# Deeper rings of split weights, shared banks combined over three tile pairs with four plain tiles last, and decay products moved from GpSimd to ScalarE in a three-block float32 model

## The reference, cut to what matters

```python
def _mlp(x, norm_g, w1, w2):              # w1: 1024 x 4096, w2: 4096 x 1024
    h = _rmsnorm(x, norm_g)
    return jnp.square(jax.nn.relu(h @ w1)) @ w2

# retention: per head a decay table, from one learned logit per head and direction
dmask = where(allowed, exp(lg * maximum(diff, 0)), 0)   # lg = log_sigmoid(decay)
a = einsum('bhid,bhjd->bhij', qc, kc) * dmask
```

## Time and profile before

| | |
|---|---|
| median of 3 runs | 979.84 us (979.39 to 979.91) |
| the profiled execution | 980.77 us, span of its instructions 979.0 us |
| mean granted TensorE clock | 0.997 |
| PE busy | 963.0 us, 98% |
| DVE busy | 776.1 us, 79% |
| ACT busy | 599.2 us, 61% |
| POOL busy | 168.5 us, 17% |
| DMA | 174.82 MB, mean 179 GB/s |

### The profile page before, as it was taken

One profiled execution on the slowest core, in us unless ns is written; L12 is line 12 of the kernel. 1 busy time (PEld: TensorE's weight loads), 2 busy tenths in 40 slices (PEclk: granted clock), 3 DMA queues, 4 the chain that ended last, 5 costly groups with the idle time before them and its releaser, 6 DMA issues.

```text
span 979.0 us, 15251 instructions
## 1 busy us (share of the span) xinstructions
PE 963.0 (98%) x5810; PEld 845.5 (86%) x5810; DVE 776.1 (79%) x1161; ACT 599.2 (61%) x987; POOL 168.5 (17%) x189
## 2 busy tenths in 40 slices
PE   9999999999998999999999999999999999999997
PEld 8878899988997888888889999998888888998885
DVE  6788678999878676786668888888767998878884
ACT  6688666556675564444447765665545867766662
POOL 2741017990000202320001000000550110000000
PEclk9999999999999999999999999999999999999999
DMA  9985545565555554435555656564545463644631
GB/s 338 302 218 194 175 129 177 182 201 194 192 175 170 189 196 154 150 130 176 189 195 172 199 176 208 193 216 145 181 161 170 133 212 94 205 133 129 215 129 44
DMA packets 110345, 174.82 MB, mean 179 GB/s; under 512 B 4289, under 2 KB 73025, under 8 KB 110273
## 3 DMA queue, kind: packets, MB, share of 16 engines
q1 hardware_dynamic: 109840, 173.40, 53.9%
q10 hardware_dynamic: 432, 0.44, 0.1%
HBM read 172.78 MB, written 1.05 MB: 178 GB/s over the span
## 4 chain that ended last, share of the span: by engine, by line
PE 90%; DVE 7%; issue 1%; ACT 0%; POOLq 0%; POOL 0%; DVEq 0%; ACTq 0%
PE ps L467 20%; PE ps L468 19%; PE ps L469 19%; PE ps L527 8%; PE ps L574 7%; PE ps L525 5%; DVE wlo L1638 3%; PE ps L543 2%; PE ps L738 1%; PE ps L718 1%; PE ps L524 1%; PE ps L541 1%; PE ps L706 1%; PE ps L662 1%; DVE arena L1765 1%
## 5 line engine op out<-in xcount | busy, mean ns | idle before, releaser
L1638 DVE TENSOR_TENSOR wlo<-raw,whi 128x1024 fp32r<-128x1024 f32 (+1 forms) x312 | 366.7, 1203 | 42.8 <-ACT whi L1105 33.1
L1105 ACT ACTIVATE whi<-raw 128x1024 fp32r<-128x1024 f32 (+1 forms) x312 | 307.2, 1023 | 41.8 <-PE ps L469 18.9
L467 PE MATMUL ps<-hT,whi 128*128 128x256 f32 x584 | 165.8, 284 | 0.3 <-issue 0.3
L469 PE MATMUL ps<-hT,wlo 128*128 128x256 f32 x584 | 165.2, 283 | 0.0
L468 PE MATMUL ps<-hT,whi 128*128 128x256 f32 x584 | 165.2, 283 | 0.0
L467 PE MATMUL ps<-whi,hT 128*128 128x512 f32 (+1 forms) x312 | 122.0, 391 | 0.9 <-DVE hT L1720 0.9
L469 PE MATMUL ps<-whi,hT 128*128 128x512 f32 (+1 forms) x312 | 120.0, 385 | 0.0
L468 PE MATMUL ps<-wlo,hT 128*128 128x512 f32 (+1 forms) x312 | 119.9, 384 | 0.0
L527 PE MATMUL ps<-hT,whi 128*128 128x512 f32 x336 | 119.8, 396 | 0.0
L467 PEld LDWEIGHTS ps<-hT,whi 128*128 128x128 f32 x584 | 111.5, 191 | 2.7 <-issue 1.4
L468 PEld LDWEIGHTS ps<-hT,whi 128*128 128x128 f32 x584 | 111.6, 191 | 1.2
(11 more groups left out here) (253 smaller groups left out, 1700.0 us busy)
## 6 DMA issues: line engine op xcount, KB each, us to landing
raw<-in_w SPq DMA_DIRECT2D x64, 1024.0 KB, 5.4
raw<-in_w_in SPq DMA_DIRECT2D x34, 1024.0 KB, 5.2
raw<-in_w_in_o SPq DMA_DIRECT2D x24, 1024.0 KB, 5.1
raw<-in_w_out_o SPq DMA_DIRECT2D x8, 1024.0 KB, 5.0
raw<-in_w_in_e SPq DMA_DIRECT2D x5, 1024.0 KB, 12.8
raw<-in_w_mem SPq DMA_DIRECT2D x4, 1024.0 KB, 10.3
raw<-in_w_out_e SPq DMA_DIRECT2D x4, 1024.0 KB, 5.0
raw<-in_w_out SPq DMA_DIRECT2D x4, 1024.0 KB, 5.0
```

Of the source, the lines that this page charges most:

```text
L467: e.matmul(o, a[0], b[0], start=start, stop=False)
L469: return e.matmul(o, a[1], b[0], start=False, stop=stop)
L1105: e.activation(split_half(i)[0], raw_half(i), ACT.Copy).then_inc(*up("hi", ("hi", i)))
L1638: e.tensor_tensor(l, raw_half(i), h.bitcast(F32), ALU.subtract).then_inc(*up("lo", ("lo", i)))
```

## The change

It does five things:

1. The rings get 7 buffers each (from 6 high and 5 low). `HI_AHEAD` goes from 5 to 6, `LO_AHEAD` from 4 to 6. The 12 KB per partition come from the DMA scratch, which is set to 1024 bytes.
2. The `seven` tiles are now 1, 2, 3, 5, 6, 7, 9, 10, 11: three in a row and not two. `four` are 0, 4, 8. The plain tiles are 12 to 15 (`PLAIN = 12`).
3. `sums_shared` is cut in three parts, done at j = 12, 13 and 14, and not all at j = 14.
4. The 16 decay products move from POOL to ACT, four at each of j = 5 to 8.
5. POOL's 8 decay sums wait for ACT's products one by one (`dsc`).

```diff
-NRAW, NHI, NLO = 4, 6, 5
-HI_AHEAD, LO_AHEAD = 5, 4
+NRAW, NHI, NLO = 4, 7, 7
+HI_AHEAD, LO_AHEAD = 6, 6
-SEVEN = (1, 2, 4, 5, 7, 8, 10, 11, 13)
+SEVEN = (1, 2, 3, 5, 6, 7, 9, 10, 11)
+PLAIN = 12
...
-                    elif p == 14:
-                        take("acc", stage, 1)
+                    elif p >= PLAIN:
+                        if p == PLAIN:
+                            take("acc", stage, 1)
                         for x in range(2):
-                            acc_half(stage, ("w2", layer, p), x, ur1(p), 0, fresh=() if x else (1,))
+                            acc_half(stage, ("w2", layer, p), x, ur1(p), 0, fresh=(1,) if (p, x) == (PLAIN, 0) else ())
...
+                if 5 <= j < 9:
+                    for h in (2 * j - 10, 2 * j - 9):
+                        w.wait_ge(*at("dlo"))
+                        e.activation(dtab[:, h, :], cst[:, C_U:C_U + 384], ACT.Copy, scale=lgt[:, 96 + h:97 + h])
+                        e.activation(dtmp[:, h, :], cst[:, C_L:C_L + 384], ACT.Copy, scale=lgt[:, 104 + h:105 + h]).then_inc(
+                            *up("aev", ("dsc", h)))
...
-                    if j == SEVEN[-1] + 1:
-                        sums_shared(stage)
+                    if PLAIN <= j < PLAIN + 3:
+                        sums_shared(stage, j - PLAIN)
...
                 for h in range(8):
-                    e.tensor_scalar(dtab[:, h, :], cst[:, C_U:C_U + 384], lo[:, h:h + 1], None, ALU.mult)
-                    d = e.tensor_scalar(dtmp[:, h, :], cst[:, C_L:C_L + 384], lo[:, 8 + h:9 + h], None, ALU.mult)
-                chained(d, 7)
-                for h in range(8):
+                    w.wait_ge(*at("dsc", h))
                     e.tensor_tensor(dtab[:, h, :], dtab[:, h, :], dtmp[:, h, :], ALU.add).then_inc(*up("po", ("dtab", h // 2)))
...
-    nc = bacc.Bacc("TRN2", target_bir_lowering=False, num_devices=1)
+    nc = bacc.Bacc("TRN2", target_bir_lowering=False, num_devices=1, dynamic_dma_scratch_size=1024)
```

More of the change, by code:

```diff
@@ L359, in slots @@
         def slots(p):
-            return (1, 8) if p in SEVEN else (0, 4) if p >= 14 else (0, 6)
+            return (1, 8) if p in SEVEN else (0, 4) if p >= PLAIN else (0, 6)
         def place(key, i):
@@ L1385, in u_high @@
                 k0, k1 = slots(j)
-                w.wait_ge(*at("sq2", layer, j) if j >= 14 else at("us", layer, j))
+                w.wait_ge(*at("sq2", layer, j) if j >= PLAIN else at("us", layer, j))
                 if j >= 2:
@@ L2043, in u_low, with sums_shared @@
                     *up("xl", ("ul", layer, j)))
-            def sums_shared(stage):
+            def sums_shared(stage, part):
                 b1, b5, b6, b7 = (bank("acc", stage, n) for n in ("b1", "b5", "b6", "b7"))
@@ L2051, in sums_shared @@
                 v, w_, y, z = (VW[:, i, :] for i in range(4))
[L2052 to L2063, removed]
@@ L2064, in sums_shared @@
-                e.scalar_tensor_tensor(x0, w_, ri[0], x0, ALU.mult, ALU.add).then_inc(*up("fs", ("f7", stage)))
-                w.wait_ge(*at("f5", stage))
-                e.scalar_tensor_tensor(x1, y, ri[0], x1, ALU.mult, ALU.add).then_inc(*up("fs", ("f8", stage)))
+                if part == 0:
+                    w.wait_ge(*at("accs", stage))
+                    e.tensor_copy(z, b6).then_inc(*up("fs", ("f0", stage), ("free", ("acc", stage, "b6"))))
+                    w.wait_ge(*at("f0", stage))
+                    e.tensor_tensor(v, b1, z, ALU.subtract).then_inc(*up("fs", ("f1", stage)))
+                    w.wait_ge(*at("f1", stage))
+                    e.tensor_tensor(w_, v, b7, ALU.subtract).then_inc(*up("fs", ("f2", stage), ("free", ("acc", stage, "b7"))))
+                elif part == 1:
+                    e.scalar_tensor_tensor(x2, b1, ri[1], x2, ALU.mult, ALU.add).then_inc(
+                        *up("fs", ("f3", stage), ("free", ("acc", stage, "b1"))))
+                    w.wait_ge(*at("f2", stage))
+                    e.tensor_tensor(z, b5, v, ALU.subtract).then_inc(*up("fs", ("f4", stage)))
+                    e.tensor_tensor(y, b5, w_, ALU.subtract).then_inc(*up("fs", ("f5", stage), ("free", ("acc", stage, "b5"))))
+                else:
+                    w.wait_ge(*at("f5", stage))
+                    e.scalar_tensor_tensor(x3_, z, ri[1], x3_, ALU.mult, ALU.add).then_inc(*up("fs", ("f6", stage)))
+                    e.scalar_tensor_tensor(x0, w_, ri[0], x0, ALU.mult, ALU.add).then_inc(*up("fs", ("f7", stage)))
+                    e.scalar_tensor_tensor(x1, y, ri[0], x1, ALU.mult, ALU.add).then_inc(*up("fs", ("f8", stage)))
@@ L2076, in mlp @@
                         weights_to(i + 1 + LO_AHEAD)
-                    if j < 14:
+                    if j < PLAIN:
                         u_sums(layer, j)
@@ L2465, in decays @@
                 chained(e.tensor_scalar(lo, d, 0.0, None, ALU.min), 5)
-                chained(e.tensor_tensor(lo, lo, pl, ALU.subtract), 6)
+                e.tensor_tensor(lo, lo, pl, ALU.subtract).then_inc(*up("po", ("dlo",)))
                 for h in range(8):
-                    e.tensor_scalar(dtab[:, h, :], cst[:, C_U:C_U + 384], lo[:, h:h + 1], None, ALU.mult)
-                    d = e.tensor_scalar(dtmp[:, h, :], cst[:, C_L:C_L + 384], lo[:, 8 + h:9 + h], None, ALU.mult)
-                chained(d, 7)
-                for h in range(8):
+                    w.wait_ge(*at("dsc", h))
                     e.tensor_tensor(dtab[:, h, :], dtab[:, h, :], dtmp[:, h, :], ALU.add).then_inc(*up("po", ("dtab", h // 2)))
```

## The result

| | before | after |
|---|---|---|
| median | 979.88 us (4 runs, 979.39 to 979.95) | 1006.22 us (4 runs, 1005.66 to 1007.14) |
| the profiled execution, its span | 980.77, 979.0 us | 1005.66, 1003.8 us |
| mean granted TensorE clock | 0.997 | 0.991 |

The ratio is 1.0271 with a 95% interval of 1.0253 to 1.0289: 26.3 us slower. The forecast was 5.7 us slower. Its sign was right, its size too small by more than a factor of four, and the time lies outside its range.

The account below looks back on a forecast made before the run. The prediction took PE, busy for 98% of the span, to bound the kernel, so the change counted through waits. Its terms, 8.8 + 4.4 - 7.5 = + 5.7 us, gave 985.5 us, range 982.5 to 989.

Parts of the forecast that it names:

- The chain through ACT: MLPs, between `u_sums` and `u_low`: DVE idles 1.4 us for ACT's high part, making PE late; 8.8 us in both layers.
- a rival of 0.04: The clock falls in every row's wait, six times 1.7 us, 10 more: 995 us; chance 0.04.
- a slow PE gives DVE the time of the next wait: Tiles 7 and 8 of layer 0: after a long wait, a slow PE gives DVE the time the next wait would take.
- POOL's sums: Layer 0 MLP, j = 5 to 8: each sum takes 0.8 us from DVE, costing 4.4 us in all, from 0 to 8.4.
- the rule of the Trainium skill: GpSimd and VectorE take a shared port pair as an exclusive lock; by it the 4.4 us would be 8.3.
- The products on ACT: Layer 0, four per step, 2 us, hidden by ACT's 4.7 us idle: cost 0; without this cover, 2 us.
- What was removed: Old waits at the last tiles, at 218 us with its slow clock, and at 158 us go: 7.5 us together.
- those at the last tiles: Both layers, tiles 14 and 15: waits for `wlo` and `u_low` go with `sums_shared` in three parts, 2.8 us.
- the 0.3 us at 158 us: PE's wait at 158 us goes, as DVE is two halves further: 0.3 us.
- The first rival: All waits go and none comes: 972.3 us; chance 0.17.
- The signs that the prediction named: PE waits some 1.4 us before tiles 3, 7, 11, longer in layer 0; DVE idles behind `u_sums`; old waits gone.
- The wait of 218 us with its low clock: Layer 0: PE's 2.74 us wait and the slow clock's 1.7 us go as products leave POOL, 4.4 us.

Follow-up runs that it names:

- e12: Changed kernel with LO_AHEAD 6 only outside the two MLPs and 5 in them: 989.32 us, ratio 1.0095 to the kernel before.
- e9: Changed kernel with LO_AHEAD 6 in the two MLPs only and 5 elsewhere: 989.93 us, ratio 1.0099 to the kernel before.
- e10: e9 with each of POOL's eight decay sums one column wide and not 384: 987.12 us, ratio 1.0071 to the kernel before.
- e3: Changed kernel with LO_AHEAD 5 for 6, nothing else: 972.16 us, ratio 0.9916 to the kernel before.
- e8: Changed kernel with LO_AHEAD 4 for 6: 973.66 us, ratio 0.9934 to the kernel before.
- e11: Changed kernel with rings of 8 high and 6 low buffers and distances 7 and 5: 972.78 us, ratio 0.9925 to the kernel before.
- e2: Kernel before with rings of 7 and 7, both distances 6 and the small DMA scratch: 1007.88 us, ratio 1.0289.
- e1: Kernel before with rings of 7 and 7 and the small DMA scratch, distances still 5 and 4: 977.13 us, ratio 0.9969.
- e4: Changed kernel with rings 6 and 5, distances 5 and 4 and the full DMA scratch: 974.15 us, ratio 0.9937 to the kernel before.
- e7: Kernel before with only the new tiles, plain tiles and `sums_shared` in three parts: 982.11 us, ratio 1.0019.
- e5: Kernel before with both distances 5, six low buffers for five and the small DMA scratch: 1002.07 us, ratio 1.0216.

## Why the prediction was wrong, point by point

**The step that failed** is what it did not count: it worked the new distances out in the MLPs only. It said that the waits between an MLP and the next stage are left alone and had no term for the attention stages at all, although `HI_AHEAD` and `LO_AHEAD` hold for every weight of the program. Measured there: 17.2 us (e12) instead of 0. That is most of the 20.6 us by which it was short. The order of the changed kernel showed it without a run: ahead of the reciprocal stands a low part whose high part stands, on ACT, behind the exponentials.

**The chain through ACT** was right in mechanism and, at tiles 3, 7 and 11, in size: 1.35 us from start to start against 1.4. Two things were missing. Tile 0 of each layer loses 1.35 as well, as the additions moved ahead of its `u_sums`; the forecast began to follow the tiles at tile 1. And a clock fall behind the longest wait, 1.6 us, was held for a rival of 0.04 and for all six rows; it came in one. Nor did waits "of some 2 us on" decide it, as that rival had it: behind the same wait of 2.23 us the clock stayed up in e9. There the wait ahead of tile 8 was 2.21 us, against 0.62 in the changed kernel, where PE was slow just before; which fits the prediction's remark that a slow PE gives DVE the time of the next wait. Chain and POOL's sums were to cost 8.8 + 4.4 = 13.2 us. In the changed kernel's trace the two MLPs lose some 15.6 with the clock, and e9 over e3, in medians, 17.8.

**POOL's sums** were given 4.4 us and cost 2.8 in the MLP with equal distances (e10). What a sum takes from DVE was sized right: in e9's trace two of them add 1.6 us to a step (`u_low` and the low part behind it, above), the 0.8 each of the forecast. What was wrong is that PE has to wait for all of it. By the rule of the Trainium skill that the prediction weighed ("SBUF — State Buffer", section "SBUF: two separate sides": the later of the two engines is blocked until the first ends) they would, by the prediction's estimate, have cost 8.3; DVE was slowed, as the rule's direction has it, but far from blocked. The products on ACT, taken as free, are the other part: without the sums layer 0 still loses 2.4 us more than layer 1 (e10). ACT's idle time was to cover them, but the high part that DVE wants next stands behind them. Sums and products together make layer 0 lose 4.8 us more than layer 1 in the changed kernel, clock included (10.2 against 5.4), so the total of 4.4 + 0 was near by luck. In e3, with a lag of one half, PE has no wait at all at these steps.

**What was removed** was nearly right, but only for a lag of one half: 7.5 us forecast, 8.1 measured (e3 against its own kernel before, 980.25), and in e3 all the waits named are gone. In the changed kernel those at the last tiles and the 0.3 us at 158 us are gone, and the one ahead of tile 7 of layer 0 is not. The first rival, that all waits go and none comes, gave 972.3; e3, which has every part of the change but one number, took 972.16. It was the right account of a kernel with a lag of one half.

**The sum by measured terms**: 17.8 in the MLPs and 17.2 outside, less 8.1, is 26.9, where 26.3 was measured. None of the rivals described this.

**The signs that the prediction named**: waits at tiles 3, 7 and 11 of both layers, longer ones in layer 0, the idle of DVE behind `u_sums`, and the end of the waits at the last tiles came. The wait of 218 us with its low clock did not go: 2.23 us and a slow stretch stand ahead of the same tile. The signs confirmed a part and said nothing of the whole, since none of them looked outside the MLPs.

## What to carry to other kernels

When two engines work through one list of pieces in program order, the second reading what the first makes, keep the second at least one piece behind the first: here that one piece was worth 34 us of 1006, and a second one nothing (e8, e11). A look-ahead constant holds in every stage that uses it, so read the order around the latest wait of each stage, not only of the one that the change is about. Deeper rings are worth nothing if both sides run equally far ahead (e2), and were worth 2 to 3 us where the lag was kept (e1, and e3 against e4). And a part that loses alone (e7) can gain beside another (e4).

## What the runs showed of the hardware

- How long PE waits did not by itself decide whether its clock fell. Behind seven waits of 1.18 to 1.30 us in the changed kernel the granted clock stayed at 1.00. At a wait of 4.07 us it fell to 0.50 (mean 0.57 over the next 6.77 us). In between both came: the same 2.23 us ahead of tile 7 of layer 0 had a clock of 0.53 behind it in the changed kernel and of 1.00 in e9, where the clock fell at the next wait, 2.21 us. In e5 the clock stayed at 1.00 behind waits of 2.40 and 2.66 us and read 0.51 behind another of 2.66. A fall behind such a wait cost 1.6 to 1.7 us; behind 2.56 us in e1 the 0.50 lasted some 6.7 us and not 3.4. The two stretches of e9 (length, busy of PE, PEld, DVE, ACT, POOL, granted clock, DMA share, GB/s), the first behind the wait of 2.23 us, the second behind that of 2.21:

```profile
223.70:227.10 3.40, 3.40 (x15) 2.83 (x16) 3.40 (x3) 3.37 (x5) 0.74 (x1) 1.00 0.05 18
236.90:240.30 3.40, 3.40 (x9) 2.62 (x9) 3.40 (x4) 0.73 (x1) 0.00 (x0) 0.50 0.31 83
```

- Eight GpSimd sums of 128x384 cost the end of the kernel 2.8 us (e9 less e10), though VectorE's 128x1024 instructions take 2.0 us and not 1.2 beside them, low parts and weight additions alike (the rows of e7).
